# High and low parts of a pair's four weight sums made by one instruction each, in a two-block transformer kernel

## The chip, the cores and the metric

The kernel runs on one core of one Trainium2 chip. The metric is the device time of one execution in microseconds. TensorE (PE) multiplies, VectorE (DVE) and ScalarE (ACT) prepare operands and read results, SyncE (SP) issues the transfers.

## The reference

The reference is one token batch of 256 tokens and model width 2048 through two different blocks, all in float32. What matters here is the feed-forward part at the end of each block (inner width 5632):

```python
v = rmsnorm(h, ffn_norm_w[l])
h = h + (jax.nn.silu(v @ w_gate[l]) * (v @ w_up[l])) @ w_down[l]
...
gate, up = jnp.split(h @ w_ffn_in[l], 2, axis=-1)
x = x + rms_norm((jax.nn.silu(gate) * up) @ w_ffn_down[l], norm_ffn_post[l])
```

Ahead of it stand, in the first block, a state-space mixer and a sparse attention, and in the second a gated recurrence and a forgetting attention. The change touches neither.

## The kernel before

**Units.** Every weight matrix is streamed from HBM in units of 128 x 1024 floats (512 KB), numbered through the whole program; SP loads unit j into buffer `raw[j % 5]`. To multiply in float32 with a fast matmul type, each unit is split: ACT rounds it to the high part (`whi`, line 1313), DVE subtracts that from the raw weights to get the low part (`wlo`, line 1927), and PE adds up three products, low x high, high x high and high x low (`three`, line 597 through `mm`). There are four slots of `whi` and `wlo`: ACT may write unit j when PE has done with unit j - 4 (`slot_free`).

**Steps.** Each engine has its own program, written as a walk over the same units. At step g, PE multiplies unit g; ACT does `split_to(ahead(g))`, that is it splits unit g + 3, then `split_sums(g)`, then side work; DVE does `sums(g)`, `split_to(ahead(g))` (low part of unit g + 3), `split_sums(g)`, then side work. Each engine's instructions run strictly in that order. Semaphores hold the engines together: `s_hi` counts high parts, `s_lo` low parts, `s_unit` units that PE has read.

**Items and pairs.** An item is 16 units with one set of output banks. In the feed-forward parts most items are of the kind "duo": two chunks of 512 output columns at once, unit 2p from the one chunk and 2p + 1 from the other, for the same two tiles of the contraction. In some unit pairs p of such an item (`SEVEN` = 1, 3, 5, in two items of a block `FEWER` = 1, 5, and `DOWN` = 3, 5 in the items of the down projection) the 2 x 2 block product is made from seven products instead of eight. These pairs need four sums of weight tiles, `Tf[:, 0..3, :]`, each 128 x 512 (a region of `scr` in the first block and of `h` in the second, which are the names that rows show), and the high and low parts of these sums, `tsp[:, 0]` and `tsp[:, 1]` (a region of `spare`). Say a pair's second unit is U. Then, before the change:

- DVE, step U - 5: sums 0 and 1 (one instruction of 1024, or two of 512; line 1976).
- DVE, step U - 3: sums 2 and 3 (rows `scr<-raw,scr` or `h<-raw,h`, x2), then the low part of unit U (`wlo` 128x512: of a pair's second unit half is split), then the low parts of the sums (`spare<-scr,spare` or `spare<-h,spare`, two of 128x1024).
- ACT, step U - 3: high part of unit U, then the high parts of sums 0 and 1 (`spare<-scr` or `spare<-h` 128x1024) and, when sum 3 is there, of sums 2 and 3. At the first step of an item two gate instructions follow (`scr<-scr,sm` or `h<-h,sm`, x2).
- PE, unit U (15 matmuls of 512 columns): three with the unit's own weights (`whi,spare` and `wlo,spare`), then nine (row `ps<-spare`) and three (`ps<-spare,xx`) with the sums. Of the nine the first and second read high parts of sum 0, the third is the first that reads a low part; the sums 2 and 3 come from the seventh on.

`s_ts` counts the sums (three steps a pair), `s_th` their high parts and `s_tl` their low parts, both twice a pair; `s_T` tells that PE has done with a pair's sums.

Of the pair's first unit PE runs 6 matmuls, of a unit outside such pairs 12. A feed-forward part holds ten gate and up items (`fu1` to `fu10`, of which `fu4` and `fu8` have two such pairs and the others three) and four down items with two pairs each, in the order fu1 to fu4, fd0_0, fd0_2, fu5 to fu8, fd1_0, fd1_2, fu9, fu10: 36 pairs, and 72 in the whole program. After the last pair of an item DVE reads four results of it (`corrections`: `h<-ps,h` 128x512 x4), which begin when ACT has copied the first.

Of the kernel before, what the change touches and what calls it, by code (L numbers as in the profile page):

```python
# [172 lines left out]
def build(nc, ins, out):  # L173
    F = mybir.dt.float32
# [5 lines left out]
    MUL, ADD, SUB, MAX, MIN = ALU.mult, ALU.add, ALU.subtract, ALU.max, ALU.min  # L180
# [6 lines left out]
    with ctx:  # L187
# [3 lines left out]
        def sem(name):  # L191
            return ctx.enter_context(nc.semaphore(name))
# [22 lines left out]
        ps = ctx.enter_context(nc.psum_tensor("ps", [P, 8, 512], F))  # L215
# [25 lines left out]
        def bc(ap, axis, shape):  # L241
            return ap.unsqueeze(axis).to_broadcast(shape)

        def two(ap):
            return ap.rearrange("p (a b) -> p a b", a=2)
# [44 lines left out]
        def ffn_work(b, o, n):  # L290
            return (scr if b == 1 else h)[:, :, :].rearrange("p a b -> p (a b)")[:, o:o + n]
# [3 lines left out]
        Tf = [None] + [ffn_work(b, 0, 2048).rearrange("p (t x) -> p t x", t=4) for b in (1, 2)]  # L295
# [4 lines left out]
        tsp = spare[:, 1, :, :].rearrange("p (a t) c -> p a (t c)", a=2).rearrange("p a (t c) -> p a t c", t=4)  # L300
# [106 lines left out]
        s_ts, s_th, s_tl, s_T = sem("s_w_sums"), sem("s_w_sums_hi"), sem("s_w_sums_lo"), sem("s_seven_done")  # L407
# [60 lines left out]
        def slot(q):  # L468

            if turn <= q < turn + NSPL:  # L470
                return spare[:, 0, q % NSPL, :], spare[:, 1, q % NSPL, :]
            return whi[:, q % NSPL, :], wlo[:, q % NSPL, :]

        def sums_of(j):

            odd = 0 <= j < len(units) and units[j]["u"] % 2 == 1
            return units[j]["seven"] if odd else None
# [41 lines left out]
        def layer(j):  # L519
            return int(units[j]["item"]["name"][0])  # L520
# [54 lines left out]
        def tensor(e):  # L575
            on = Waits(e)
# [14 lines left out]
            def claim(*banks):  # L591
                for b in banks:
                    if b in freed:
                        on.wait_ge(*freed[b])

            def mm(o, l, r, start=True, stop=True, skip=False):
                return e.matmul(o, l, r, start=start, stop=stop, skip_group_check=skip)  # L597
# [65 lines left out]
            def three(o, x, w, start, stop, ready):  # L663
                mm(o, x[1], w[0], start=start, stop=False)
                mm(o, x[0], w[0], start=False, stop=False)
                on.wait_ge(*ready)
                return mm(o, x[0], w[1], start=False, stop=stop)

            def duo_unit(i, it, u):

                p, side, d = u // 2, u % 2, it["d"]
                q = it["first"] + u
                n0, s0 = place[i], 4 - place[i]
                if u == 0:
                    claim(*range(n0, n0 + 4))
                s_oh, s_ol, f0 = fill_of(it["name"])
                w = slot(q)
                x = [[[v[:, k, tb * 128:tb * 128 + 128] for v in ((hhi, hlo) if it["op"] == "h" else (xhi, xlo))] for tb in range(2)] for k in it["ks"][p]]
                on.wait_ge(s_hi, q + 1)
                on.wait_ge(s_oh, f0 + it["ks"][p][1] + 1)  # L680
                on.wait_ge(s_ol, f0 + it["ks"][p][1] + 1)
                n = units[q]["seven"]
                if n is None:
                    for kk in range(2):
                        c0 = 512 - 512 * kk
                        for tb in range(2):
                            m = three(ps[:, n0 + 2 * side + tb, :], x[kk][tb], [a[:, c0:c0 + 512] for a in w],
                                      u < 2 and kk == 0, p == KT // 2 - 1 and kk == 1, (s_lo, q + 1))
                    m.then_inc(s_unit, 1)
                    return  # L690
                j = n - it["s0"]
                jx = (SEVEN if it["op"] == "x" else DOWN).index(p)
                a, z = j == 0, j == len(it["sevens"]) - 1
                low, high = [[v[:, c0:c0 + 512] for v in w] for c0 in (0, 512)]
                sx = [[Sx[it["op"]][jx][:, v, t, :] for v in range(2)] for t in range(4)]
                tw = [[tsp[:, v, t, :] for v in range(2)] for t in range(4)]
                if side == 0:
                    if a:
                        claim(*range(s0, s0 + 4))
                    three(ps[:, s0, :], x[0][0], high, a, z, (s_lo, q + 1))  # L700
                    three(ps[:, n0, :], x[1][0], low, False, False, (s_lo, q + 1)).then_inc(s_unit, 1)
                    return
                nx = sums_at(it) + jx
                on.wait_ge(s_sxh, nx + 1)
                on.wait_ge(s_sxl, nx + 1)
                three(ps[:, n0 + 2, :], sx[3], low, False, False, (s_lo, q + 1)).then_inc(s_unit, 1)
                on.wait_ge(s_th, 2 * n + 1)
                three(ps[:, s0 + 1, :], sx[0], tw[0], a, z, (s_tl, 2 * n + 1))
                three(ps[:, s0 + 3, :], sx[2], tw[1], a, z, (s_tl, 2 * n + 1))
                on.wait_ge(s_th, 2 * n + 2)  # L710
                three(ps[:, s0 + 2, :], sx[1], tw[2], a, z, (s_tl, 2 * n + 2))
                three(ps[:, n0 + 1, :], x[1][1], tw[3], False, False, (s_tl, 2 * n + 2)).then_inc(s_T, 1)
                if z:
                    freed[s0] = (s_e11, d + 1)
                    for b in range(s0 + 1, s0 + 4):
                        freed[b] = (s_e, d + 1)
# [589 lines left out]
        def scalar(e):  # L1306
            on, own = Waits(e), Own(s_a)
# [4 lines left out]
            def act(o, i, f=ACT.Copy, **kw):  # L1312
                return e.activation(o, i, f, **kw)  # L1313
# [27 lines left out]
            def split_sums(g):  # L1341

                n7 = sums_of(g + 3)
                if n7 is not None:
                    on.wait_ge(s_T, n7)
                    on.wait_ge(s_ts, 3 * n7 + 1)
                    tf = Tf[layer(g + 3)]
                    act(tsp[:, 0, 0:2, :], tf[:, 0:2, :]).then_inc(s_th, 1)
                    on.wait_ge(s_ts, 3 * n7 + 3)
                    act(tsp[:, 0, 2:4, :], tf[:, 2:4, :]).then_inc(s_th, 1)  # L1350

            def tick():
                for g in list(running):
# [566 lines left out]
        def vector(e):  # L1920
            on, own = Waits(e), Own(s_v)
# [4 lines left out]
            def tt(o, a, b, op):  # L1926
                return e.tensor_tensor(o, a, b, op)  # L1927
# [36 lines left out]
            def sums(g):  # L1964

                n7 = sums_of(g + 5)
                if n7 is not None:
                    tf = Tf[layer(g + 5)]
                    ra, rb = (g + 4) % NRAW, (g + 5) % NRAW
                    on.wait_ge(s_raw[ra], 16 * ((g + 4) // NRAW + 1))  # L1970
                    on.wait_ge(s_raw[rb], 16 * ((g + 5) // NRAW + 1))
                    on.wait_ge(s_tl, 2 * n7)
                    second_ = raw[:, rb, 512:1024]
                    if rb:
                        both_ = raw[:, ra:rb + 1, :].rearrange("p a b -> p (a b)")[:, 512:1536]
                        tt(tf[:, 0:2, :], two(both_), bc(second_, 1, [P, 2, 512]), SUB).then_inc(s_ts, 1)
                    else:
                        tt(tf[:, 0, :], raw[:, ra, 512:1024], second_, SUB)
                        tt(tf[:, 1, :], raw[:, rb, 0:512], second_, SUB).then_inc(s_ts, 1)
                n7 = sums_of(g + 3)  # L1980
                if n7 is not None:
                    tf = Tf[layer(g + 3)]
                    on.wait_ge(s_ts, 3 * n7 + 1)
                    tt(tf[:, 2, :], raw[:, (g + 3) % NRAW, 0:512], tf[:, 0, :], ADD).then_inc(s_ts, 1)
                    on.wait_ge(s_ts, 3 * n7 + 2)
                    tt(tf[:, 3, :], raw[:, (g + 2) % NRAW, 0:512], tf[:, 2, :], SUB).then_inc(s_ts, 1)

            def split_sums(g):

                n7 = sums_of(g + 3)  # L1990
                if n7 is not None:
                    tf = Tf[layer(g + 3)]
                    for t in range(2):
                        on.wait_ge(s_th, 2 * n7 + t + 1)
                        on.wait_ge(s_ts, 3 * n7 + 1 + 2 * t)
                        tt(tsp[:, 1, 2 * t:2 * t + 2, :], tf[:, 2 * t:2 * t + 2, :], tsp[:, 0, 2 * t:2 * t + 2, :].bitcast(F), SUB).then_inc(s_tl, 1)

            def tick():
                for g in list(running):
# [1251 lines left out]
```

## Time and profile before

| | |
|---|---|
| median of 3 runs | 2511.02 us (2510.28 to 2512.76) |
| span of the profiled execution | 2506.6 us |
| what lies around the span (median less span) | 4.4 us |
| PE busy | 2495.7 us (100%) |
| DVE busy | 1958.2 us (78%) |
| ACT busy | 1363.3 us (54%) |
| DMA queue of the weights | 65.5% of 16 engines |

Times are from the span's start. A busy PE is not PE at its peak: matmuls overlap, so a row's duration is longer than the distance from one start to the next. The time of the profiled execution is not listed apart; the 4.4 us are the distance from its span to the median.

### The profile page before, as it was taken

What the parts mean: (1) busy time and instruction counts of PE and PEld (TensorE: products, weight loads), DVE (VectorE), ACT (ScalarE), POOL (GpSimd) and SP (SyncE); (2) the same over time, 40 slices, a digit from 0 to 9 for tenths busy, and PEclk for the clock granted to TensorE, in tenths of its full rate; (3) what the DMA queues carried; (4) which work ended last, traced back from release to release, by engine and by line L of the source; (5) the groups of instructions that cost most, each with busy time, mean ns of one, the idle gap of its engine ahead of it and who ended that gap; (6) DMA issues with size and microseconds to landing.
All of it is one profiled execution on the core that took longest, in us unless ns stands there. A gap on an engine that the chain in (4) does not pass through costs nothing.

```text
span 2506.6 us, 33781 instructions
## 1 busy us (share of the span) xinstructions
PE 2495.7 (100%) x13224; PEld 2077.6 (83%) x13224; DVE 1958.2 (78%) x2426; ACT 1363.3 (54%) x1766; POOL 53.6 (2%) x68
## 2 busy tenths in 40 slices
PE   9999999999999999999999999999999999999998
PEld 9878878888888888888888888888878888888887
DVE  6787777998899889776578554566689988998886
ACT  5575645555555555566455454534555545554553
POOL 0161000000000000000000000000000000000000
PEclk9999999999999999999999999999999999999999
DMA  8654557676757675776655556776576776677665
GB/s 306 182 161 125 169 164 236 214 252 202 235 185 252 196 241 180 242 225 219 192 171 169 166 173 192 227 252 216 178 259 209 236 227 206 205 235 226 204 204 188
DMA packets 175856, 521.38 MB, mean 208 GB/s; under 512 B 17297, under 2 KB 50321, under 8 KB 174385
## 3 DMA queue, kind: packets, MB, share of 16 engines
q1 hardware_dynamic: 175552, 519.07, 65.5%
q8 instruction: 105, 1.72, 0.3%
q14 instruction: 55, 0.44, 0.1%
q10 hardware_dynamic: 144, 0.15, 0.0%
HBM read 495.68 MB, written 23.07 MB: 207 GB/s over the span
## 4 chain that ended last, share of the span: by engine, by line
PE 95%; DVE 3%; ACT 1%; issue 1%; DMA 0%; DVEq 0%; ACTq 0%
PE ps L597 94%; PE ps L601 1%; DVE wlo L1927 1%; DVE scr L1927 1%; ACT whi L1313 1%; DVE h L1930 0%; DVE spare L1927 0%; DVE h L1927 0%; DMA raw<-in_gu 0%; DVE scr L1930 0%; DMA raw<-in_w_in 0%; ACT L1313 0%; ACT scr L1313 0%; ACT W L1313 0%; ACT h L1313 0%
## 5 line engine op out<-in xcount | busy, mean ns | idle before, releaser
L1927 DVE TENSOR_TENSOR wlo<-raw,whi 128x1024 fp32r<-128x1024 f32 x884 | 1032.6, 1180 | 449.4 <-ACT whi L1313 445.3
L1313 ACT ACTIVATE whi<-raw 128x1024 fp32r<-128x1024 f32 x884 | 882.9, 1019 | 614.9 <-PE ps L597 577.9
L597 PE MATMUL ps<-whi,xx 128*128 128x512 f32 x3488 | 1077.7, 390 | 0.0
L597 PEld LDWEIGHTS ps<-whi,xx 128*128 128x128 f32 x3488 | 651.6, 188 | 135.3 <-issue 1.4
L597 PE MATMUL ps<-wlo,xx 128*128 128x512 f32 x1744 | 679.7, 390 | 0.5 <-DVE wlo L1927 0.5
L597 PEld LDWEIGHTS ps<-wlo,xx 128*128 128x128 f32 x1744 | 327.3, 188 | 71.4 <-DVE wlo L1927 3.0
L597 PE MATMUL ps<-whi,hlo 128*128 128x512 f32 (+1 forms) x856 | 332.8, 389 | 0.1
L597 PE MATMUL ps<-wlo,hhi 128*128 128x512 f32 (+1 forms) x856 | 331.5, 387 | 0.3 <-DVE wlo L1927 0.3
L597 PE MATMUL ps<-whi,hhi 128*128 128x512 f32 (+1 forms) x856 | 331.4, 387 | 0.0
L597 PE MATMUL ps<-xx,whi 128*128 128x512 f32 (+1 forms) x1088 | 310.8, 372 | 0.6 <-ACT xx L1313 0.5
L597 PEld LDWEIGHTS ps<-xx,wlo 128*128 128x128 f32 x960 | 180.4, 188 | 37.2 <-DVE wlo L1927 0.3
L597 PE MATMUL ps<-xx,wlo 128*128 128x256 f32 x960 | 199.1, 279 | 0.1
L597 PEld LDWEIGHTS ps<-wlo,hhi 128*128 128x128 f32 x856 | 160.7, 188 | 33.7 <-DVE wlo L1927 0.7
L597 PEld LDWEIGHTS ps<-whi,hlo 128*128 128x128 f32 x856 | 160.7, 188 | 33.4 <-PE ps L597 0.5
L597 PEld LDWEIGHTS ps<-whi,hhi 128*128 128x128 f32 x856 | 160.8, 188 | 32.3
L597 PEld LDWEIGHTS ps<-xx,whi 128*128 128x128 f32 x1088 | 166.3, 189 | 4.0 <-issue 2.3
L1313 ACT ACTIVATE spare<-scr 128x1024 fp32r<-128x1024 f32 (+1 forms) x75 | 77.7, 1041 | 115.3 <-DVE scr L1927 104.4
L1313 ACT ACTIVATE spare<-h 128x1024 fp32r<-128x1024 f32 (+1 forms) x75 | 77.5, 1040 | 111.1 <-DVE h L1927 96.9
L597 PE MATMUL ps<-spare 128*128 128x512 f32 (+2 forms) x520 | 130.2, 390 | 0.3 <-DVE spare L1927 0.3
L597 PEld LDWEIGHTS ps<-spare 128*128 128x128 f32 x520 | 97.4, 188 | 21.0 <-DVE spare L1927 1.2
L1927 DVE TENSOR_TENSOR spare<-scr,spare 128x1024 fp32r<-128x1024 f32 (+1 forms) x75 | 86.8, 1198 | 0.5 <-ACT spare L1313 0.4
L1927 DVE TENSOR_TENSOR spare<-h,spare 128x1024 fp32r<-128x1024 f32 (+1 forms) x75 | 86.8, 1198 | 0.5 <-ACT spare L1313 0.4
(208 smaller groups left out, 1843.5 us busy)
## 6 DMA issues: line engine op xcount, KB each, us to landing
raw<-in_gu SPq DMA_DIRECT2D x352, 512.0 KB, 4.4
raw<-in_w_in SPq DMA_DIRECT2D x256, 512.0 KB, 4.0
raw<-in_dn SPq DMA_DIRECT2D x176, 512.0 KB, 4.3
raw<-in_w_out SPq DMA_DIRECT2D x32, 512.0 KB, 3.6
W<-blocks SPq DMA_DIRECT2D x128, 128.0 KB, 3.8
raw<-in_w_up SPq DMA_DIRECT2D x32, 512.0 KB, 4.3
raw<-in_w_o SPq DMA_DIRECT2D x32, 512.0 KB, 4.3
blocks<-h SPq DMA_DIRECT2D x16, 512.0 KB, 5.3
```

The costliest lines, as they stand in the source:

```text
L597: return e.matmul(o, l, r, start=start, stop=stop, skip_group_check=skip)
L601: return e.transpose(o, i, C("ident")[0:k, 0:k])
L1313: return e.activation(o, i, f, **kw)
L1927: return e.tensor_tensor(o, a, b, op)
```

## The change

The high parts of all four sums are made by one ACT instruction of 128 x 2048, which waits for the last sum. The low parts are made by one DVE instruction of 128 x 2048, at step U - 2 in place of U - 3. The counters `s_th` and `s_tl` now go up once a pair, so PE waits for the whole before the first use.

```diff
@@ duo_unit (PE)
-                on.wait_ge(s_th, 2 * n + 1)
-                three(ps[:, s0 + 1, :], sx[0], tw[0], a, z, (s_tl, 2 * n + 1))
-                three(ps[:, s0 + 3, :], sx[2], tw[1], a, z, (s_tl, 2 * n + 1))
-                on.wait_ge(s_th, 2 * n + 2)
-                three(ps[:, s0 + 2, :], sx[1], tw[2], a, z, (s_tl, 2 * n + 2))
-                three(ps[:, n0 + 1, :], x[1][1], tw[3], False, False, (s_tl, 2 * n + 2)).then_inc(s_T, 1)
+                on.wait_ge(s_th, n + 1)
+                three(ps[:, s0 + 1, :], sx[0], tw[0], a, z, (s_tl, n + 1))
+                three(ps[:, s0 + 3, :], sx[2], tw[1], a, z, (s_tl, n + 1))
+                three(ps[:, s0 + 2, :], sx[1], tw[2], a, z, (s_tl, n + 1))
+                three(ps[:, n0 + 1, :], x[1][1], tw[3], False, False, (s_tl, n + 1)).then_inc(s_T, 1)
@@ split_sums (ACT)
-                    on.wait_ge(s_ts, 3 * n7 + 1)
-                    tf = Tf[layer(g + 3)]
-                    act(tsp[:, 0, 0:2, :], tf[:, 0:2, :]).then_inc(s_th, 1)
                     on.wait_ge(s_ts, 3 * n7 + 3)
-                    act(tsp[:, 0, 2:4, :], tf[:, 2:4, :]).then_inc(s_th, 1)
+                    act(tsp[:, 0, :, :], Tf[layer(g + 3)]).then_inc(s_th, 1)
@@ sums (DVE)
-                    on.wait_ge(s_tl, 2 * n7)
+                    on.wait_ge(s_tl, n7)
@@ split_sums (DVE)
-                n7 = sums_of(g + 3)
+                n7 = sums_of(g + 2)
                 if n7 is not None:
-                    tf = Tf[layer(g + 3)]
-                    for t in range(2):
-                        on.wait_ge(s_th, 2 * n7 + t + 1)
-                        on.wait_ge(s_ts, 3 * n7 + 1 + 2 * t)
-                        tt(tsp[:, 1, 2 * t:2 * t + 2, :], tf[:, 2 * t:2 * t + 2, :], tsp[:, 0, 2 * t:2 * t + 2, :].bitcast(F), SUB).then_inc(s_tl, 1)
+                    on.wait_ge(s_th, n7 + 1)
+                    on.wait_ge(s_ts, 3 * n7 + 3)
+                    tt(tsp[:, 1, :, :], Tf[layer(g + 2)], tsp[:, 0, :, :].bitcast(F), SUB).then_inc(s_tl, 1)
```

DVE around the second pair of item fu2 of the first block, before. `wlo 128x512` is the low part of unit U, the `wlo 128x1024` behind the sums that of unit U + 1:

```order
538 L1927 TENSOR_TENSOR wlo<-raw,whi 128x1024 [waits s_hi] x2
539 L1927 TENSOR_TENSOR scr<-raw,scr 128x512 [waits s_w_sums] x2
540 L1927 TENSOR_TENSOR wlo<-raw,whi 128x512 [waits s_hi]
541 L1927 TENSOR_TENSOR spare<-scr,spare 128x1024 [waits s_w_sums_hi]
542 L1927 TENSOR_TENSOR spare<-scr,spare 128x1024 [waits s_w_sums,s_w_sums_hi]
543 L1927 TENSOR_TENSOR wlo<-raw,whi 128x1024 [waits s_hi]
544 L1927 TENSOR_TENSOR scr<-raw 128x1024 [waits s_w_sums_lo,s_raw4,s_raw3]
```

The same place on DVE now:

```order
535 L1923 TENSOR_TENSOR wlo<-raw,whi 128x1024 [waits s_hi] x2
536 L1923 TENSOR_TENSOR scr<-raw,scr 128x512 [waits s_w_sums] x2
537 L1923 TENSOR_TENSOR wlo<-raw,whi 128x512 [waits s_hi]
538 L1923 TENSOR_TENSOR wlo<-raw,whi 128x1024 [waits s_hi]
539 L1923 TENSOR_TENSOR spare<-scr,spare 128x2048 [waits s_w_sums,s_w_sums_hi]
540 L1923 TENSOR_TENSOR scr<-raw 128x1024 [waits s_w_sums_lo,s_raw4,s_raw3]
```

The low parts of the sums have moved behind the low part of unit U + 1, which waits for that unit's high part.

ACT at the first pair of the same item, before:

```order
377 L1313 ACTIVATE whi<-raw 128x512 [waits s_unit,s_raw1]
378 L1313 ACTIVATE spare<-scr 128x1024 [waits s_w_sums] x2
379 L1313 ACTIVATE scr<-scr,sm 128x512 [waits s_corrected]
380 L1313 ACTIVATE scr<-scr,sm 128x512
381 L1313 ACTIVATE whi<-raw 128x1024 [waits s_unit,s_raw2]
```

ACT at that place now:

```order
375 L1312 ACTIVATE whi<-raw 128x512 [waits s_unit,s_raw1]
376 L1312 ACTIVATE spare<-scr 128x2048 [waits s_w_sums]
377 L1312 ACTIVATE scr<-scr,sm 128x512 [waits s_corrected]
378 L1312 ACTIVATE scr<-scr,sm 128x512
379 L1312 ACTIVATE whi<-raw 128x1024 [waits s_unit,s_raw2]
```

The order of ACT's work is kept; the high part of unit U + 1 (`whi` 128x1024) still stands behind the high parts of the sums and, at an item's first pair, behind the two gates.

## Rows read from the trace of the kernel before

**Rows 1.** The page: busy time, share of the span and instructions

```profile
PE 2495.7 (100%) x13224; PEld 2077.6 (83%) x13224; DVE 1958.2 (78%) x2426; ACT 1363.3 (54%) x1766; POOL 53.6 (2%) x68
```

**Rows 2.** The waits of PE's weight loads: us in total, times, longest

```profile
PEld ps L597 <- DVE wlo L1927: 4.3, 12, 1.0
PEld ps L597 <- DVE spare L1927: 1.2, 2, 0.6
```

**Rows 3.** PE's timeline, item fu3 of block two: start us, us, what

```profile
1937.71 2.20 PE L597 MATMUL ps<-spare 128*128 128x512 f32 x9
...
1947.95 2.20 PE L597 MATMUL ps<-spare 128*128 128x512 f32 x9
...
1958.15 2.20 PE L597 MATMUL ps<-spare 128*128 128x512 f32 x9
```

**Rows 4.** DVE's timeline at the third pair of that item

```profile
1955.53 2.35 DVE L1927 TENSOR_TENSOR spare<-h,spare 128x1024 fp32r<-128x1024 f32 x2
1957.80 2.35 DVE L1927 TENSOR_TENSOR wlo<-raw,whi 128x1024 fp32r<-128x1024 f32 x2
1960.47 2.48 DVE L1927 TENSOR_TENSOR wlo<-raw,whi 128x1024 fp32r<-128x1024 f32 x2 [0.31 <-ACT whi L1313]
1962.87 2.73 DVE L1927 TENSOR_TENSOR h<-ps,h 128x512 f32<-128x512 f32 x4
```

**Rows 5.** ACT's timeline at the same pair

```profile
1955.04 1.06 ACT L1313 ACTIVATE spare<-h 128x1024 fp32r<-128x1024 f32 x1 [2.48 <-DVE h L1927]
1956.01 1.99 ACT L1313 ACTIVATE whi<-raw 128x1024 fp32r<-128x1024 f32 x2
```

**Rows 6.** ACT on tile spare: duration ns min/median/max, first and last start, forms

```profile
L1313 ACT ACTIVATE spare<-scr x75: 632/1062/1066, 427.3 to 1012.1; 128x1024 fp32r<-128x1024 f32 x72, 128x512 fp32r<-128x512 f32 x3
```

**Rows 7.** Groups of DVE by shape: a subtraction or addition of 2048

```profile
L1927 DVE TENSOR_TENSOR h<-h,scr 128x2048 f32<-128x2048 f32 x4 | 9.1, 2286 | 0.0
```

**Rows 8.** Groups of window 1930 to 1957: xcount | busy us, mean ns | idle before

```profile
L1927 DVE TENSOR_TENSOR h<-raw,h 128x512 f32<-128x512 f32 x6 | 4.1, 689 | 0.1
L1930 DVE SCALAR_TENSOR_TENSOR h<-h,sm 128x512 f32<-128x512 f32 x2 | 1.4, 747 | 0.0
L1313 ACT ACTIVATE h<-h,sm 128x512 f32<-128x512 f32 x2 | 1.3, 708 | 0.0
```

**Rows 9.** DVE's low parts of the sums at an item's first pair (fu3, fu8, fu9, fu1, fd1_0 of block two)

```profile
1935.81 2.35 DVE L1927 TENSOR_TENSOR spare<-h,spare 128x1024 fp32r<-128x1024 f32 x2
2228.39 2.35 DVE L1927 TENSOR_TENSOR spare<-h,spare 128x1024 fp32r<-128x1024 f32 x2
2353.48 2.36 DVE L1927 TENSOR_TENSOR spare<-h,spare 128x1024 fp32r<-128x1024 f32 x2
1853.68 2.35 DVE L1927 TENSOR_TENSOR spare<-h,spare 128x1024 fp32r<-128x1024 f32 x2
2280.41 2.35 DVE L1927 TENSOR_TENSOR spare<-h,spare 128x1024 fp32r<-128x1024 f32 x2
```

**Rows 10.** PE's matmuls on the sums at these pairs: fu8, fu9, fu1, fd1_0

```profile
2230.15 2.20 PE L597 MATMUL ps<-spare 128*128 128x512 f32 x9
2356.63 2.20 PE L597 MATMUL ps<-spare 128*128 128x512 f32 x9
1854.95 1.89 PE L597 MATMUL ps<-spare 128*128 128x512 f32 x7 [0.17 <-DVE spare L1927]
```

**Rows 11.** fu8's second pair, DVE then PE

```profile
2247.59 2.35 DVE L1927 TENSOR_TENSOR spare<-h,spare 128x1024 fp32r<-128x1024 f32 x2
...
2251.23 2.20 PE L597 MATMUL ps<-spare 128*128 128x512 f32 x9
```

**Rows 12.** Stretches at the end of the span: PE busy (x), ..., granted clock, DMA share, GB/s

```profile
2493.40:2502.80 9.40, 5.99 (x48) 5.79 (x48) 8.14 (x16) 2.33 (x8) 0.00 (x0) 1.00 0.33 118
2502.90:2506.60 3.70, 0.00 (x0) 0.00 (x0) 0.89 (x2) 0.00 (x0) 0.00 (x0) 0.50 0.71 261
```

## The prediction, made before the changed kernel was run

> **What bounds the kernel now.** I read the page first. PE is busy 2495.7 of 2506.6 us [rows 1], so nothing that only unloads DVE or ACT can give much, and anything that makes PE wait is paid in full. The next view was the waits of PE's weight loads: DVE's low parts of the weights held them for 4.3 us in all, and the low parts of the sums for 1.2 us in two waits [rows 2]. A change to how the sums are split can therefore win a microsecond or two on PE's own path. What it can lose is the slack that the present order has, and that is read in the timelines of a feed-forward item.
>
> There, PE starts a matmul of 512 columns every 0.227 us: from one pair's `ps<-spare` row to the next, 1947.95 to 1958.15, are 10.20 us for 45 matmuls (15 of unit U, 24 of the plain pair, 6 of the next pair's first unit) [rows 3]. The first low part of a sum is needed by the third matmul of that row, 0.45 us behind its start: at 1958.60 for the third pair of fu3. DVE makes these low parts from 1955.53 on, in two instructions [rows 4]; the first half, the one that PE asks for here, is there at about 1956.75, which is 1.85 us early. The other half is needed 1.36 us later and comes 1.13 us later. So the slack is one to two microseconds in a chain in which DVE has no idle time from its sums to the end of the two `wlo` rows [rows 4]. ACT stood idle 2.48 us before the second half of the high parts, waiting for DVE's last sum; it has time, but not early [rows 5].
>
> **The change, part by part.**
>
> *Fewer, larger instructions.* A DVE subtraction of 2048 takes 2.29 us [rows 7], two of 1024 together 2.35 us [rows 4]. That is 0.06 us a pair, 4 us of DVE time over 72 pairs (36 in each block, [rows 6] for the first), none of it PE's. For ACT no row shows 2048 elements. From 512 to 1024 a copy goes from 0.632 to 1.062 us [rows 6], so 2048 is estimated at 1.062 + 2 x 0.43 = 1.92 us. It can't be under 1.06 or above two of them, 2.12; I take 1.92.
> The Trainium skill, "VectorE: DVE Perf Modes", in the section on the TRN2 errata, says that VectorE and ScalarE pay a fixed extra cost for each instruction, so larger tiles are better. By that rule the change is right, and by its own reckoning the sum would be a small gain. The trace agrees on the direction, with 2.29 against 2.35 us; it doesn't say that the gain lies where PE waits.
>
> *The high parts wait for the last sum, and all that stands behind them on ACT waits too.* Before, ACT had the first half done ahead of the last sum, so from that sum on it needed one instruction (1955.04), and the high part of unit U + 1 began 0.97 us later [rows 5]. Now it needs 1.92, so `whi` of U + 1 begins 1.83 us after the last sum and ends 2.87 us after it.
>
> *The low parts stand behind `wlo` of unit U + 1.* That one waits for the `whi` just named. Before, DVE reached it only after both halves of the sums, when the high part was long there; the queue had no gap. Now DVE comes to it 0.5 us after the last sum, with `wlo` of U done, and stands for about 2.3 us. Then follow `wlo` at 1.14 us from start to start (half of a x2 row less its overlap, [rows 4]) and the low parts, 2.29 us.
> From ACT's start to the low parts: 2.87 + 0.03 (semaphore) + 1.14 + 2.29 = 6.33 us. ACT's second half began 0.49 us before DVE's `spare` row (1955.04 and 1955.53, [rows 4, 5]). So the low parts would end 5.84 us behind the start of today's `spare` row, and with 0.05 for PE to see it 5.9 us. At an item's first pair ACT has the two gates ahead of `whi` [rows 8], worth 1.23 us net of overlap: 7.13 us.
>
> *What PE then waits,* pair by pair, is `spare` row start + 5.9 (or 7.13) - third matmul:
>
> - First pair after an item of full pairs (fu3): 1935.81 + 7.13 - 1938.16 = 4.8 us [rows 3, 9]. The same pair has DVE a little ahead of today after the previous item: PE's wait at that item's third pair ends with DVE free, and three `wlo` of 1.14 behind PE's 1958.60 let the reading of the results begin at 1962.0 and not 1962.87 [rows 4]. I take 0.8 off: 4.0.
> - Second pair. After a wait DVE is behind PE and not paced by it: the high parts that it needs next hang on units that PE finished before its wait. So low parts to low parts is DVE's own work plus the 6.33: gates 1.4, sums 0 and 1 1.2, two `wlo` 2.3, sums 2 and 3 1.3 [rows 4, 8], together 6.0 with overlaps, that is 12.4 us against PE's 10.2: 2.2 us more.
> - Third pair: the same without the gates, 4.7 + 6.4 = 11.1 against 10.2: 0.9 us.
> - Ten items are of this kind (fu2, fu3, fu6, fu7, fu10, twice): 7.1 us each, 71 us.
> - fu4 and fu8, twice: 2228.39 + 7.13 - 2230.60 = 4.9, less 0.8; the second pair stands alone, 2247.59 + 5.9 - 2251.68 = 1.8 [rows 9 to 11]. 5.9 x 4 = 24 us.
> - fu5 and fu9, twice, behind down items and without gates: 2353.48 + 5.9 - 2357.08 = 2.3, then 0.9 and 0.9 [rows 9, 10]. 4.1 x 4 = 16 us.
> - fu1, twice: 1853.68 + 5.9 - 1854.95 = 4.6, then 0.9 and 0.9 [rows 9, 10]. 6.4 x 2 = 13 us.
> - fd0_0 and fd1_0, twice: 2280.41 + 5.9 - 2283.64 = 2.7, then 0.9 [rows 9, 10]. 3.6 x 4 = 14 us.
> - fd0_2 and fd1_2, twice: between 0 and the 0.9 of a pair that follows another; 0.5 x 4 = 2 us.
>
> The sum is 140 us on 2506.6 + 4.4, the median of the runs: **2651 us**, 5.6% slower. Nothing gives a wait back, since PE is busy elsewhere. The transfers don't enter: the raw buffers are freed by sums 2 and 3 and by `wlo`, which are not moved behind anything.
>
> **Rivals.**
>
> - *The waits add up in full.* If DVE is paced by PE also within an item, every later pair begins where it does today, plus PE's delay. The third pair then costs 1955.53 + 5.9 - 1958.60 = 2.8 and not 0.9 [rows 3, 4], the second, between it and the first, about 3.8 and not 2.2: 3.5 us more in ten items, and 2 to 3 more in the ten that have a following pair without gates. 2651 + 35 + 20 = 2706 us. Against it speaks that DVE's rows of a pair follow each other without idle time [rows 4]. Chance 0.08.
> - *Only the first pair of an item pays.* If DVE makes up the following ones, 10 x 4.0 + 4 x 5.9 + 2 x 4.6 + 4 x 2.3 + 4 x 2.7 = 93 us are left: 2604 us. For it would speak idle time of DVE in the pairs that I have not seen. Chance 0.07.
> - *The clock.* TensorE's granted clock is 1.00 up to 2502.80 with PE's last matmuls in that stretch, and 0.50 in the last 3.7 us, with none [rows 12]; that is 2.4 and 1.2 GHz. The new waits at first pairs in sixteen items are between 4 and 5 us without a matmul. If the clock falls in them and comes back only after the rest of the unit, ten matmuls of twice 0.227 us, that is 2.3 us each, 36 us; in ten of the items the second pair's wait of 2.2 us is DVE's and swallows it. So 14 to 36 us more, 2665 to 2687 us. Chance 0.15.
>   The Trainium skill, "TensorE: Matmul & The Clock Gate", Part 1, says that an idle stretch brings the clock back to 1.2 GHz and sustained work lifts it again. The trace agrees at its end; no row of it shows a wait of this length inside the program, so which of the sixteen would fall is open.
> - *Not slower.* The low parts have always been ready early, only the fixed costs change, and the kernel is the same or 1 to 4 us faster: 2507 to 2511 us. This needs today's `spare` row to start at least 5.9 us ahead of the third matmul. In the seven places shown it is between 1.3 and 4.1 us ahead [rows 3, 4, 9 to 11]. Chance 0.03.
>
> **How the numbers follow.** The mechanism with my sizes has 0.67, the four rivals 0.08, 0.07, 0.15 and 0.03. The likeliest gives 2651; its own range, from ACT's 2048 at 2.12 (0.2 more on 58 waits, +12) and the 0.8 not taken off (+11) down to waits 20% shorter (-28), is 2623 to 2674. The range of 8 in 10 takes in the clock above and part of the case below: 2612 to 2692. A measurement of this kernel can tell about 0.2%, 5 us, from no change. Faster by more 0.01, within it 0.02, slower 0.97.
>
> **What would show it.** In the changed profile: `spare` of ACT at 1.9 us and of DVE at 2.29 us; PE's idle time put down to DVE `spare`, 140 us in 60 waits or more, with the longest between 4 and 5.5 us, at first pairs; DVE idle before a `wlo` in such a pair for about 2.3 us, ended by ACT's `whi`, 3.5 with the gates; and pair distances on PE of 12.4 and 11.1 us where they are 10.2 today. The granted clock tells of the third rival. I am wrong if PE's waits on `spare` stay under 20 us, or if ACT's `whi` of U + 1 runs ahead of the high parts of the sums.

## The result

The changed kernel takes 2675.39 us (median of 4 runs, 2673.53 to 2676.41) against 2510.97 us (4 runs) before: a ratio of 1.0653, 95% interval 1.064 to 1.0666, or 164 us slower. The forecast was 2651 us, in a range of 2612 to 2692.

The page of the changed kernel, busy time by engine, and the chain that ended last:

```profile
span 2674.6 us, 33637 instructions
...
PE 2555.4 (96%) x13224; PEld 2107.4 (79%) x13224; DVE 1955.3 (73%) x2354; ACT 1354.0 (51%) x1694; POOL 53.6 (2%) x68
...
PE 75%; DVE 13%; issue 6%; ACT 5%; DMA 0%; DVEq 0%; ACTq 0%; SPq 0%
```

DVE and ACT have 72 instructions fewer each, DVE 2.9 us and ACT 9.3 us less busy time than in [rows 1]. PE is busy for 60 us longer with the same 13224 matmuls, and idle for the rest of the difference; both need an explanation.

The waits of PE and of its weight loads (us in total, times, longest us), where [rows 2] had 1.2 us in two waits for `spare`:

```profile
PE ps L597 <- DVE spare L1923: 106.5, 50, 4.3
...
PEld ps L597 <- DVE spare L1923: 127.9, 51, 4.8
```

So nearly all of PE's new idle time is one wait, for the low parts of the sums. How it comes about is read in item fu3 of block two, DVE first (start us, us, what, idle before), to be held against [rows 4]:

```profile
2035.83 0.68 DVE L1923 TENSOR_TENSOR wlo<-raw,whi 128x512 fp32r<-128x512 f32 x1
2040.07 1.22 DVE L1923 TENSOR_TENSOR wlo<-raw,whi 128x1024 fp32r<-128x1024 f32 x1 [3.55 <-ACT whi L1312]
2041.21 2.29 DVE L1923 TENSOR_TENSOR spare<-h,spare 128x2048 fp32r<-128x2048 f32 x1
2043.41 1.41 DVE L1926 SCALAR_TENSOR_TENSOR h<-h,sm 128x512 f32<-128x512 f32 x2
...
2052.54 1.23 DVE L1923 TENSOR_TENSOR wlo<-raw,whi 128x1024 fp32r<-128x1024 f32 x1 [2.39 <-ACT whi L1312]
2053.69 2.28 DVE L1923 TENSOR_TENSOR spare<-h,spare 128x2048 fp32r<-128x2048 f32 x1
2056.10 1.29 DVE L1923 TENSOR_TENSOR h<-raw 128x512 f32<-128x512 f32 x2
...
2063.98 1.23 DVE L1923 TENSOR_TENSOR wlo<-raw,whi 128x1024 fp32r<-128x1024 f32 x1 [2.38 <-ACT whi L1312]
2065.12 2.29 DVE L1923 TENSOR_TENSOR spare<-h,spare 128x2048 fp32r<-128x2048 f32 x1
```

ACT in the same pairs:

```profile
2035.95 1.92 ACT L1312 ACTIVATE spare<-h 128x2048 fp32r<-128x2048 f32 x1 [3.94 <-DVE h L1923]
2037.77 1.32 ACT L1312 ACTIVATE h<-h,sm 128x512 f32<-128x512 f32 x2
2038.99 3.45 ACT L1312 ACTIVATE whi<-raw 128x1024 fp32r<-128x1024 f32 x4
...
2049.65 1.92 ACT L1312 ACTIVATE spare<-h 128x2048 fp32r<-128x2048 f32 x1 [7.20 <-DVE h L1923]
2051.47 1.04 ACT L1312 ACTIVATE whi<-raw 128x1024 fp32r<-128x1024 f32 x1
```

And PE:

```profile
2038.82 0.39 PE L597 MATMUL ps<-spare 128*128 128x512 f32 x1
2043.55 3.36 PE L597 MATMUL ps<-spare 128*128 128x512 f32 x7 [4.34 <-DVE spare L1923]
...
2055.84 2.20 PE L597 MATMUL ps<-spare 128*128 128x512 f32 x9
...
2067.47 0.73 PE L597 MATMUL ps<-spare 128*128 128x512 f32 x2 [0.81 <-DVE spare L1923]
```

In order of time: ACT's one instruction begins after the last sum and takes 1.92 us; at the first pair its two gates follow; only then comes `whi` of unit U + 1, the first of the four in that row, which ends at 2040.03. DVE, done with `wlo` of U at 2036.5, has stood 3.55 us for it, makes `wlo` of U + 1, and after that the low parts, until 2043.50. PE starts its third matmul at 2043.55. In the second and third pair DVE stands 2.4 us.

Seven matmuls took 3.36 us behind that first wait, and nine 2.20 us in the next pair. The windows show why (busy and count of PE, PEld, DVE, ACT, POOL; then granted clock, DMA share, GB/s):

```profile
2000.00:2041.80 41.80, 37.91 (x165) 30.42 (x163) 31.70 (x31) 22.54 (x22) 0.00 (x0) 1.00 0.65 205
2041.80:2048.60 6.80, 5.05 (x12) 3.99 (x13) 6.80 (x7) 0.65 (x2) 0.00 (x0) 0.50 0.35 92
2048.70:2091.00 42.30, 39.33 (x172) 31.87 (x171) 32.17 (x34) 22.11 (x22) 0.00 (x0) 1.00 0.67 209
```

The granted clock was 0.50, 1.2 GHz, from within the wait to 2048.6. So the second pair has no wait left (its nine matmuls take 2.20 us and no idle time stands before them): PE comes to it late because its own matmuls were slow. Over both feed-forward parts the clock averages 0.96:

```profile
440.00:1100.00 660.00, 606.28 (x2533) 490.25 (x2531) 522.68 (x524) 309.82 (x307) 0.00 (x0) 0.96 0.62 192
1930.00:2600.00 670.00, 615.02 (x2581) 497.28 (x2581) 528.46 (x526) 311.42 (x309) 0.00 (x0) 0.96 0.61 192
```

That is 0.04 of 1330 us, 53 us of matmul work not done at the full clock, or some 106 us at half of it. Whether it is part of the 164 us needs an experiment, since a slow matmul may only fill a wait.

### The profile page after: what moved, and what is told of

Same layout as the page of the kernel before. It is cut to its first block, busy times and chain, and to the rows that moved or that the text cites. A ratio compares the mean times of both kernels' runs of the same rounds, so it can differ in the third digit from the quotient of the medians.

```text
span 2674.6 us, 33637 instructions
## 1 busy us (share of the span) xinstructions
PE 2555.4 (96%) x13224; PEld 2107.4 (79%) x13224; DVE 1955.3 (73%) x2354; ACT 1354.0 (51%) x1694; POOL 53.6 (2%) x68
## 4 chain that ended last, share of the span: by engine, by line
PE 75%; DVE 13%; issue 6%; ACT 5%; DMA 0%; DVEq 0%; ACTq 0%; SPq 0%
PE ps L597 74%; DVE spare L1923 6%; DVE wlo L1923 3%; ACT whi L1312 3%; DVE scr L1923 2%; DVE h L1923 2%; ACT spare L1312 1%; PE ps L601 1%; DVE h L1926 0%; ACT h L1312 0%; ACT scr L1312 0%; DMA raw<-in_w_in 0%; DVE scr L1926 0%; ACT L1312 0%; ACT W L1312 0%
## 5 line engine op out<-in xcount | busy, mean ns | idle before, releaser
L597 PE MATMUL ps<-spare 128*128 128x512 f32 (+2 forms) x520 | 167.9, 458 | 93.7 <-DVE spare L1923 92.0
L597 PEld LDWEIGHTS ps<-spare 128*128 128x128 f32 x520 | 109.6, 218 | 134.4 <-DVE spare L1923 110.0
L1312 ACT ACTIVATE spare<-h 128x2048 fp32r<-128x2048 f32 (+1 forms) x39 | 70.9, 1818 | 168.6 <-DVE h L1923 168.6
L1312 ACT ACTIVATE spare<-scr 128x2048 fp32r<-128x2048 f32 (+1 forms) x39 | 70.9, 1818 | 167.0 <-DVE scr L1923 167.0
L1923 DVE TENSOR_TENSOR spare<-h,spare 128x2048 fp32r<-128x2048 f32 (+1 forms) x39 | 84.3, 2162 | 0.0
L1923 DVE TENSOR_TENSOR spare<-scr,spare 128x2048 fp32r<-128x2048 f32 (+1 forms) x39 | 84.3, 2161 | 0.0
```

## The experiments

Each is compared with the kernel before as it was timed beside it (2511 to 2512 us). The first three each apply one part of the change to the kernel before. Lines of code that aren't shown are marked with three dots or named below.

**Order alone.** DVE's two halves of the low parts a step later, nothing merged:

```diff
-                n7 = sums_of(g + 3)
+                n7 = sums_of(g + 2)
                 if n7 is not None:
-                    tf = Tf[layer(g + 3)]
+                    tf = Tf[layer(g + 2)]
                     for t in range(2):
```

> The kernel before with one edit: DVE makes the two halves of the low parts at step U - 2, behind wlo of unit U + 1; ACT's halves and all counters stay. Theory (the chain over ACT's whi and DVE's wlo of U + 1 is what costs): the first low half ends about 4.4 us after the last sum, at a first pair with gates 5.7 us, against 1.7 before; PE's waits then are 2.8 us at the 14 first pairs with gates, 1.3 at the second, 0.1 at the third: 65 us in all, and up to 25 more if the granted clock falls in the waits of 2.8 us. 2576 to 2601 us. Rival (the larger instructions alone cost, since the whole must be there before the first use): within 10 us of the kernel before.

Measured: 2597.20 us, ratio 1.0345 (1.0328 to 1.0363), 86 us slower, inside the range that the theory gave with the clock. DVE at the first and the second pair of fu3 of block two:

```profile
1992.84 1.23 DVE L1927 TENSOR_TENSOR wlo<-raw,whi 128x1024 fp32r<-128x1024 f32 x1 [2.70 <-ACT whi L1313]
...
2004.48 1.22 DVE L1927 TENSOR_TENSOR wlo<-raw,whi 128x1024 fp32r<-128x1024 f32 x1 [1.47 <-ACT whi L1313]
```

The stand behind `whi` of U + 1 is there without any larger instruction. The rival is out.

**ACT's instruction alone.**

```diff
-                    on.wait_ge(s_ts, 3 * n7 + 1)
-                    tf = Tf[layer(g + 3)]
-                    act(tsp[:, 0, 0:2, :], tf[:, 0:2, :]).then_inc(s_th, 1)
                     on.wait_ge(s_ts, 3 * n7 + 3)
-                    act(tsp[:, 0, 2:4, :], tf[:, 2:4, :]).then_inc(s_th, 1)
+                    act(tsp[:, 0, :, :], Tf[layer(g + 3)]).then_inc(s_th, 1)
```

(with `s_th` counted once a pair by DVE and PE)

> The kernel before with one edit: the high parts of the four sums by one ACT instruction; DVE's two halves stay at step U - 3. Theory: the first low half ends 3.2 us after the last sum in place of 1.7, which takes 1.5 us from slacks of 0.8 to 1.4 at first pairs and 0.05 at fu1; with about 1 us at second pairs, 18 us in all, no fall of the clock: 2529 us (2518 to 2545). Rival (the 0.86 us by which ACT's whi of U + 1 comes later is the main cost): 2580 us or more.

Measured: 2562.61 us, ratio 1.0205 (1.019 to 1.022): 51 us slower where I expected 18, outside my range, and short of the rival's 2580. DVE's timeline of fu3's second and third pair:

```profile
1983.13 2.36 DVE L1923 TENSOR_TENSOR spare<-h,spare 128x1024 fp32r<-128x1024 f32 x2 [1.44 <-ACT spare L1312]
...
1993.47 2.36 DVE L1923 TENSOR_TENSOR spare<-h,spare 128x1024 fp32r<-128x1024 f32 x2 [1.44 <-ACT spare L1312]
```

The idle time of 1.44 us is what the expectation implies (ACT's 1.92 and 0.03 for the semaphore, less 0.5 for `wlo` of U). DVE waits for the high parts themselves and not for ACT's `whi` of U + 1, so the rival's mechanism isn't at work. What I had wrong is how much of the idle time DVE can afford. The window from the third matmul of fu3's first pair to that of the next item's, in the kernel before:

```profile
1938.16:1979.68 41.52, 41.52 (x184) 34.30 (x183) 39.32 (x43) 23.19 (x27) 0.00 (x0) 1.00 0.70 226
```

DVE is busy 39.32 of 41.52 us: it has 2.2 us to spare in an item, not 1 or 2 us in each pair. Three stands of 1.4 us are 4.3 us, so at least 2.1 us of each full item must be paid. Matching the matmuls of the two traces one by one, the third matmuls of fu3's three pairs are later by 1.9, 1.4 and 0.1 us more each time, 3.4 us; in fu5 and fu9 none is later at all.

**DVE's instruction alone,** at the old step:

```diff
-                    for t in range(2):
-                        on.wait_ge(s_th, 2 * n7 + t + 1)
-                        on.wait_ge(s_ts, 3 * n7 + 1 + 2 * t)
-                        tt(tsp[:, 1, 2 * t:2 * t + 2, :], tf[:, 2 * t:2 * t + 2, :], ...).then_inc(s_tl, 1)
+                    on.wait_ge(s_th, 2 * n7 + 2)
+                    on.wait_ge(s_ts, 3 * n7 + 3)
+                    tt(tsp[:, 1, :, :], tf, tsp[:, 0, :, :].bitcast(F), SUB).then_inc(s_tl, 1)
```

(with `s_tl` counted once a pair by PE and by DVE's sums)

> The kernel before with one edit: the low parts by one DVE instruction at step U - 3, ACT's two halves stay. Theory: all low parts end 3.4 us after the last sum in place of 1.7 for the first half, so 1.7 us less slack, but DVE's own chain gets no longer: 18 us, 2529 us (2518 to 2545). Rival (DVE's saved 0.06 us a pair and one wait fewer count): 2507 to 2511 us.

Measured: 2527.37 us, ratio 1.0062 (1.0047 to 1.0077), as expected in size. That DVE's own chain gets no longer was wrong: it stands 0.52 us a pair here, and fu3's second pair lost another 0.4 us. At fu3's first pair:

```profile
1948.46 2.29 DVE L1927 TENSOR_TENSOR spare<-h,spare 128x2048 fp32r<-128x2048 f32 x1 [0.52 <-ACT spare L1313]
```

**Both instructions, DVE's at the old step.** This is the changed kernel with `sums_of(g + 2)` in DVE's `split_sums` back at `g + 3`.

> The changed kernel with DVE's single low-part instruction put back to step U - 3, ahead of wlo of unit U + 1; ACT and the counters as changed. Theory (what makes the change dear is that DVE's low parts stand behind ACT's whi of U + 1, not that each is one instruction): the low parts end 4.3 us after the last sum, with or without gates; against the run with ACT's instruction alone (2563 us) each first and second pair is 1.1 us later, which is about 25 us: 2586 us (2575 to 2600), and the clock hardly falls. Rival (the two larger instructions carry most of the 164 us): 2640 us or more.

Measured: 2565.58 us, ratio 1.0215 (1.0201 to 1.0229), below my range and within 3 us of ACT's instruction alone. The 25 us that I added for the later first half are not there, although the low parts do come 1.1 us later than there. What the two kernels share is DVE's idle time behind ACT's high parts, the first line from ACT's instruction alone, the second from this kernel (us in total, times, longest):

```profile
DVE spare L1923 <- ACT spare L1312: 102.0, 72, 1.4
DVE spare L1923 <- ACT spare L1312: 102.1, 72, 1.4
```

So given ACT's single instruction, DVE's costs next to nothing, and the step later costs the rest: 2675.4 less 2565.6 is 110 of the 164 us. The order alone cost 86 and the two larger instructions at the old step 54, together 140; the other 24 us come only with both.

**The wait filled with matmuls.** The changed kernel, PE's code of a pair's second unit:

```diff
+                nm_ = ...
+                if a:
+                    fill_ = 0 if nm_ in ("d0_2", "d1_2") else 9 if nm_[0] == "d" else 7 if nm_ in ("u5", "u9") else 16
+                    some = ...
+                    for _ in range(fill_):
+                        mm(ps[:, s0 + 1, :], x[0][0][0], some)
                 on.wait_ge(s_th, n + 1)
```

> The changed kernel with matmuls of no use put into PE's wait at an item's first pair: 16 of 512 columns (3.6 us), 7 in fu5 and fu9, 9 in fd0_0 and fd1_0, written to a bank that the next matmul starts anew, so that PE is never idle for more than about 1.3 us there. The result is not changed by them. Theory (the granted clock falls to half in the waits and costs some of the difference between the 140 us that the chain explains and the 165 measured): the clock stays at 1.00 in the feed-forward parts, second pairs wait 2.2 us again in place of 0 to 0.7, and the time is 2650 to 2662 us. Rival A (the clock costs half of the 102 us that it was low, 51 us): 2624 us. Rival B (the clock's loss is swallowed whole by later waits): 2675 us.

Measured: 2665.51 us, ratio 1.0613 (1.0598 to 1.0629), 3.5 us above the theory's range. (`a` is true at an item's first such pair, `nm_` is the item's name, `some` an operand that is ready.) The clock still fell in six second pairs, behind waits of 2 us, which the next run fills as well (`if a or j == 1 and nm_ in (...)`, 8 matmuls). Those are added to results in use, so that kernel's output isn't the reference's, and only its time is read:

> The run with filled waits, with 8 more such matmuls (1.8 us) in the second pair of fu2, fu3, fu6, fu7 and fu10, where it still had waits of 2.1 us and six falls of the clock. Those of second pairs are added into a bank in use, so the output of these items is not the reference's. If a fall's loss is swallowed by the wait behind it (the third pair's 1.1 us at least), the time stays within 4 us of 2665 us with the clock at 1.00 throughout; if the six falls (20.5 us at half clock) cost their half, it is 2655 us.

Measured: 2663.76 us, ratio 1.0607 (1.0591 to 1.0623). PE in fu3's second pair there (the row of eight is the filling), and the windows of both feed-forward parts:

```profile
2045.50 1.98 PE L597 MATMUL ps<-spare,xx 128*128 128x512 f32 x8
2047.31 0.61 PE L597 MATMUL ps<-spare 128*128 128x512 f32 x2
2048.08 1.89 PE L597 MATMUL ps<-spare 128*128 128x512 f32 x7 [0.15 <-DVE spare L1929]
```

```profile
440.00:1100.00 660.00, 635.82 (x2760) 514.92 (x2759) 528.91 (x531) 310.33 (x310) 0.00 (x0) 1.00 0.62 195
1920.00:2600.00 680.00, 656.64 (x2857) 532.26 (x2856) 540.55 (x542) 319.67 (x321) 0.00 (x0) 1.00 0.63 194
```

With the clock at 1.00 throughout, the kernel is 11.6 us faster than the changed one (2675.4 - 2663.8), which lost 53 us of matmul work to the clock. Four fifths of that only filled waits that would have come anyway. The filling itself delays nothing: behind all of it PE still waits. In the rows above, two matmuls on the sums start from 2047.31 on and the third not before 2048.08. The last step, from six falls to none, gave 1.8 us for 20 us at half clock.

**ACT's instruction a step later too.** The changed kernel with ACT's `split_sums` at `sums_of(g + 2)`, so `whi` of U + 1 goes ahead of the high parts of the sums:

> The changed kernel with ACT's single high-part instruction also one step later, behind whi of unit U + 1, so that DVE's wlo of U + 1 doesn't wait for it. Theory: the low parts end 4.3 us after the last sum (5.2 at first pairs with gates) in place of 6.3 (7.6), DVE's own chain falls to 9.0 to 10.3 us a pair and stops being the bound; left are 2.2 us at 14 first pairs, 2.5 at fu1 and 4 us in the down items: 44 us, and up to 20 for the clock: 2555 to 2575 us. Rival (the place of DVE's instruction is the cost, wherever ACT's stands): 2650 us or more.

Measured: 2561.50 us, ratio 1.0197 (1.018 to 1.0214): 114 us of the 164 are gone by moving ACT's instruction behind one other. The size is right, its make-up isn't quite. PE waits at every one of the 72 pairs, a little, also where it had slack. ACT, DVE and PE at fu7's third pair:

```profile
2252.99 1.06 ACT L1312 ACTIVATE whi<-raw 128x1024 fp32r<-128x1024 f32 x1 [5.01 <-PE ps L597]
2253.95 1.90 ACT L1312 ACTIVATE spare<-h 128x2048 fp32r<-128x2048 f32 x1
...
2255.88 2.29 DVE L1923 TENSOR_TENSOR spare<-h,spare 128x2048 fp32r<-128x2048 f32 x1 [0.58 <-ACT spare L1312]
...
2257.49 2.62 PE L597 MATMUL ps<-spare 128*128 128x512 f32 x9
```

Here a chain that begins at PE is longer than PE's own work: `whi` of U + 1 waits until PE has done with unit U - 3, then come the high parts of the sums and the low parts, until 2258.17, 5.2 us after 2252.99. PE has 23 matmuls from the end of U - 3 to the third on the sums, 23 x 0.227 = 5.2 us. PE's nine matmuls take 2.62 us in place of 2.20, so with the semaphores between, the chain is longer by 0.4 us. I hadn't priced this wait, and had made the first pairs too dear (1.3 us measured, 2.2 expected) in return.

**PE takes the high products first.** The changed kernel; the eight products of the sums with high parts, then the four with low parts:

```diff
-                three(ps[:, s0 + 1, :], sx[0], tw[0], a, z, (s_tl, n + 1))
-                ...
+                four = ...
+                for o, x_, w_, a_, z_ in four:
+                    mm(o, x_[1], w_[0], start=a_, stop=False)
+                    mm(o, x_[0], w_[0], start=False, stop=False)
+                on.wait_ge(s_tl, n + 1)
+                for o, x_, w_, a_, z_ in four:
+                    m = mm(o, x_[0], w_[1], start=False, stop=z_)
+                ...
```

(`four` lists output, activations, sums and flags of the four products that stood in the lines taken out)

> The changed kernel with PE taking the eight products of the sums that need high parts alone first, and the four with low parts last, so the low parts are needed 6 matmuls, 1.36 us, later. Theory (first pairs are paced by PE, the ones behind them by DVE): only waits at first and single pairs shrink, 28 x 1.36 = 38 us, and the clock falls a little less: 2622 to 2640 us. Rival (each pair's wait is set by its own slack): 58 waits, 79 us, 2596 us.

Measured: 2648.65 us, ratio 1.0543 (1.0527 to 1.0559), a gain of 27 us: 9 us short of the theory's range and far from the rival's 79. In fu3 the first pair's wait fell from 4.34 to 3.52 us, by 0.8 and not by the 1.36 us of the working; why it is less was not followed up. The third pair's wait, paced by DVE, did not shrink (0.81 us in the changed kernel, 0.95 here). First and third pair:

```profile
2025.41 1.65 PE L597 MATMUL ps<-spare 128*128 128x512 f32 x3 [3.52 <-DVE spare L1928]
...
2049.33 0.96 PE L597 MATMUL ps<-spare 128*128 128x512 f32 x3 [0.95 <-DVE spare L1928]
```

**Both.** The last two edits in one kernel:

> Both edits together, ACT's instruction behind whi of U + 1 and PE's high products first. Theory: 0.9 us is left at 14 first pairs and 1.2 at fu1, the clock doesn't fall: 2526 us (2515 to 2540). Rival (the clock or DVE's queue keeps a part): over 2550 us.

Measured: 2515.17 us, ratio 1.0015 (1.0006 to 1.0024). The single instructions of 2048 are all in it, one of ACT and one of DVE a pair, and 160 of the 164 us are gone. It is still no gain: the kernel before is faster by 0.15%.

**High products first in the kernel before.** Same edit of PE, halves and steps as before.

> The kernel before with one edit: PE takes the eight products with high parts of the sums first, the four with low parts last. Theory: PE's waits on these sums before the change are 1.5 us in all, so 1.4 us more slack gives back nothing that can be told: 2508 to 2512 us. Rival (the slack of the halves hides small losses at many pairs): 2505 us or less.

Measured: 2512.11 us, ratio 1.0001 (0.9992 to 1.001), as expected: more slack gives nothing where PE hardly waits. No version tried beats the kernel before.

## Why the prediction was right, point by point

The direction, the place and the kind of wait were right by the mechanism. The number was 24 us short, and one of its terms came out right by luck; both are taken up below.

- **What bounds it, and where the change would be paid.** Right: PE's waits on `spare` went from 1.2 us to 106.5 and 127.9 us in the two views above, in 50 and 51 waits. "140 us in 60 waits or more" was forecast, so the sign came out smaller than the loss. 22 pairs have no wait: eight had the slack, and at fourteen, all behind a first pair, PE was late by its slow matmuls; with the clock held up it waits there too.
- **Durations.** ACT's 2048 takes 1.92 us, as estimated, and DVE's 2.29. DVE stood 3.55 us at the first pair and 2.39 at the second, where 3.5 and 2.3 were forecast.
- **The first pair.** The working of 7.13 us was right: from ACT's start at 2035.95 to PE's third matmul at 2043.55 are 7.60 us, and less the 0.49 by which ACT led the old `spare` row 7.11. The 0.8 us taken off was too much. In fu3 the third matmul comes 4.73 us after the second in place of 0.23, so 4.5 us were lost against the 4.0 forecast.
- **Second and third pair.** From one pair's third matmul to the next the changed kernel gives 12.74 us (2043.55 to 2056.29, which is the row's start and two steps of 0.227) and 11.18 us (to 2067.47), against 10.24 and 10.20 before [rows 3]. That looks like the 12.4 and 11.1 forecast, but the 12.74 are slow matmuls and no wait, so it is no test of DVE's chain. The second of the filled kernels, with the clock at 1.00, is one (it is the one meant by "filled" from here on): there PE does wait at both, and the third matmuls stand at 2035.60, 2048.08 and 2059.53, 12.48 and 11.45 us apart. The mechanism holds. One part was not in the working: sums 0 and 1 of the next pair now stand directly behind the low parts and wait for them. At 2056.10 they begin 0.13 us after 2055.97, where DVE's instructions otherwise overlap by 0.08; it is 0.2 us at such a pair.
- **The term that was right by luck.** For the second pair of fu4 and fu8 1.8 us were forecast, as a wait. Neither the changed nor the filled kernel waits there. fu8 of block two in the filled one, PE then DVE:

```profile
2388.11 2.22 PE L597 MATMUL ps<-spare 128*128 128x512 f32 x9
...
2386.09 2.29 DVE L1929 TENSOR_TENSOR spare<-h,spare 128x2048 fp32r<-128x2048 f32 x1
```

  The low parts are there at 2388.38 and the third matmul starts at 2388.57. Matched with the kernel before, that pair lost 0.15 us. In the changed kernel it lost 1.6 to 3.0 us, all but the 0.15 from matmuls at half the clock. The working let DVE begin as far ahead of PE as before; in the filled kernel `wlo` of U begins 6.7 us ahead of the third matmul (at 2381.87), in the kernel before 4.7 us (2246.99 and 2251.68), which is 2.0 us more slack than was counted with.
- **The sum.** Matching the matmuls of the filled kernel one by one with those of the kernel before, a full item lost 8.1 us, fu4 and fu8 4.7, fu5 and fu9 4.8, fu1 6.8, the first down items 4.5 and the second 1.0, against 7.1, 5.9, 4.1, 6.4, 3.6 and 0.5. Times their ten, four, four, two, four and four items the differences are 10 - 5 + 3 + 1 + 4 + 2 = 15 us, which is by how much that trace's loss is above the forecast 140 (13 by the medians). ([rows 10] names fd1_0 and shows no row of it; its nine matmuls start at 2283.19 in the trace, so the 2283.64 of the working holds.) The clock adds the rest, 11.6 us by the medians, most of it in fu4 and fu8 (6.9 us in the changed kernel) and fu1 (8.0), nothing in the full items (8.1 in both). So the miss of 24 us is in about equal parts a chain taken too short and a clock left out of the likeliest case, whose own range ended at 2674.
- **The rival of the clock,** 0.15, came true in part: it fell in the wait of every one of the sixteen items that I had named, or up to 0.8 us behind it. The filled kernel puts the price at 11.6 us, just under the 14 to 36 us, and the split is the one of its lower end: swallowed in the ten full items, paid in the other six. That 2675 lies in this rival's 2665 to 2687 is half owed to the longer chain. The Trainium skill, "TensorE: Matmul & The Clock Gate", Part 1, says that an idle stretch brings 1.2 GHz. This trace agrees, with 0.50 from 2041.80 to 2048.60, which begins inside PE's wait of 4.34 us.
- **The other rivals.** "The waits add up in full" is out: in the filled kernel the third pair cost 1.2 and not 2.8 us. "Only the first pair pays" is out by the same figure. "Not slower" needed the `spare` row 5.9 us ahead.
- **The view that would have been simpler.** From first pair to first pair DVE was busy 39.32 of 41.52 us before. The same stretch in the changed kernel, and in the filled one:

```profile
2043.55:2093.17 49.62, 44.48 (x183) 35.96 (x184) 39.49 (x40) 22.66 (x22) 0.00 (x0) 0.95 0.62 190
```

```profile
2035.60:2085.24 49.64, 47.83 (x208) 38.63 (x208) 39.51 (x40) 22.45 (x22) 0.00 (x0) 1.00 0.60 193
```

  The item takes as long at a clock of 1.00 as at 0.95, so it isn't PE that sets its length. DVE does about the same work, and 8.3 us of its 10.1 us of idle time are the three stands behind `whi`. It had 2.2 us to spare, and the item grew by 8.1.

## What to carry to other kernels

Before merging two instructions, ask what the second half was waiting for and what the first half let start: here DVE's larger instruction saved 0.06 us a pair, and ACT's made DVE stand 1.4 us a pair. When an instruction is moved behind another on its own engine, it inherits all of that one's waits, and those of the engine that feeds it. DVE, at 78% over the span, had 95% in the stage that mattered; read an engine's idle time there, between two equal points of the schedule, because that is the budget for every new stand.
And test a wait with the clock held up: a slow matmul and a wait make the same delay, and only one of them is the chain that was worked out.

## What the runs showed of the hardware

- A granted clock of 0.50 came after waits of 2.1 to 2.8 us too (behind 2.77 us at fd1_0 of block two), and not after all of them. Behind this wait of fu9 in block two it stayed at 1.00 (the second row is the window):

```profile
2514.74 1.43 PE L597 MATMUL ps<-spare 128*128 128x512 f32 x5 [2.13 <-DVE spare L1923]
```

```profile
2512.00:2519.00 7.00, 4.87 (x22) 3.72 (x21) 6.83 (x7) 1.64 (x3) 0.00 (x0) 1.00 0.44 120
2227.00:2233.00 6.00, 3.80 (x10) 2.90 (x10) 5.87 (x7) 1.22 (x2) 0.00 (x0) 0.72 0.31 100
```

  The last row is the same place in fu5, with 0.72 over its 6 us. The waits are nearly the same, and what decides between them was not tried.
- A fall of the clock cost little where a wait for another engine followed: 53 us of matmul work lost to it, 11.6 us of time.
- Two DVE instructions in a row overlap by 0.08 us, and one that waits for the result of the one before it starts 0.13 us after its end, at 30 places of the changed kernel behind the low parts.
